# Weight rests kept in the ring, four first columns per input chunk, and products into an unread bank during the norms

## The reference

```
h = h + gate * rms_norm(mixer(modulate(rms_norm(h)))) 
h = h + gate * rms_norm(w_out @ (silu(g) * u))        # [g, u] = w_in @ modulate(rms_norm(h))
```

## Time and profile before

| | |
|---|---|
| median of 3 runs | 2438.59 us (2438.23 to 2444.41) |
| the profiled execution | 2446.78 us, span 2445.0 us |
| PE busy | 2272.3 us, 93% of the span |
| PE weight loads, beside the products | 2079.2 us |
| DVE busy | 1587.0 us, 65% |
| ACT busy | 1100.2 us, 45% |
| POOL busy | 127.4 us, 5% |
| mean granted TensorE clock | 0.968 |

### The profile page before, as it was taken

The page is one execution under the profiler, slowest core; times in us unless marked ns, Lnnn a source line. Parts: engine busy times, 40 slices in busy tenths (PEclk is TensorE's granted clock), DMA queues, the critical chain, the costliest instruction groups (busy, mean ns, idle before and its releaser), DMA issues.

```text
span 2445.0 us, 40728 instructions
## 1 busy us (share of the span) xinstructions
PE 2272.3 (93%) x17218; PEld 2079.2 (85%) x17218; DVE 1587.0 (65%) x2599; ACT 1100.2 (45%) x1711; POOL 127.4 (5%) x130
## 2 busy tenths in 40 slices
PE   6998999999979999989998989998999998989997
PEld 2664878998769998979998879997678998988997
DVE  3388666646955545886556575557967656687555
ACT  2424444444164346644335453334545334836333
POOL 0013000000000000000000000005620000000000
PEclk9999999999979999999999889999999999999999
DMA  7358164552225554314453225542034553513551
GB/s 324 121 215 317 55 231 148 190 186 86 75 103 190 180 183 155 138 70 173 179 183 138 104 100 189 181 152 87 1 116 148 184 190 139 189 52 121 183 181 67
DMA packets 50293, 368.41 MB, mean 151 GB/s; under 512 B 5568, under 2 KB 5696, under 8 KB 5824
## 3 DMA queue, kind: packets, MB, share of 16 engines
q1 hardware_dynamic: 49968, 363.72, 40.9%
q10 hardware_dynamic: 144, 2.10, 0.2%
HBM read 364.75 MB, written 1.05 MB: 150 GB/s over the span
## 4 chain that ended last, share of the span: by engine, by line
PE 79%; DVE 14%; ACT 3%; issue 3%; DMA 1%; SPq 0%; DVEq 0%; ACTq 0%
PE psum L240 67%; DVE weight_parts L226 2%; PE psum L3722 1%; PE psum L3723 1%; DMA weight_ring<-stream_dram 1%; PE psum L2532 1%; DVE work L998 1%; DVE work L2839 1%; DVE work L993 1%; ACT weight_parts L197 1%; DVE work L2853 1%; PE psum L3740 1%; DVE work L2841 1%; PE psum L3017 1%; PE psum L2205 1%
## 5 line engine op out<-in xcount | busy, mean ns | idle before, releaser
L240 PE MATMUL psum<-input_parts,weight_parts 128*128 128x256 f32 x8640 | 1062.8, 286 | 45.3 <-DVE input_parts L1006 29.1
L240 PEld LDWEIGHTS psum<-input_parts,weight_parts 128*128 128x128 f32 x8640 | 1055.4, 193 | 55.3 <-issue 48.7
L226 DVE TENSOR_TENSOR weight_parts<-weight_ring,weight_parts 128x1024 fp32r<-128x1024 f32 x536 | 631.7, 1220 | 268.1 <-ACT weight_parts L197 267.1
L197 ACT ACTIVATE weight_parts<-weight_ring 128x1024 fp32r<-128x1024 f32 x540 | 541.2, 1051 | 270.0 <-PE psum L240 269.2
L240 PE MATMUL psum<-hidden_parts,weight_parts 128*128 128x256 f32 x3744 | 455.3, 283 | 10.5 <-DVE hidden_parts L2658 6.6
L240 PEld LDWEIGHTS psum<-hidden_parts,weight_parts 128*128 128x128 f32 x3744 | 449.4, 189 | 14.3 <-issue 8.8
L1080 ACT ACTIVATE work<-psum 128x256 f32<-128x256 f32 x132 | 50.7, 384 | 427.7 <-PE psum L240 427.7
L1087 DVE TENSOR_TENSOR work<-work,psum 128x256 f32<-128x256 f32 x132 | 55.6, 421 | 287.6 <-ACT work L1080 287.6
L240 PE MATMUL psum<-work,weight_ring 128*128 128x256 f32 (+1 forms) x608 | 174.8, 446 | 4.0 <-ACT work L540 2.2
L240 PEld LDWEIGHTS psum<-work,weight_ring 128*128 128x128 f32 x608 | 117.4, 195 | 57.9 <-issue 41.9
L240 PE MATMUL psum<-weight_ring,silu_cond 128*32 128x256 f32 x768 | 53.6, 408 | 25.3 <-DMA weight_ring<-stream_dram 19.3
(11 more groups left out here) (459 smaller groups left out, 2230.5 us busy)
## 6 DMA issues: line engine op xcount, KB each, us to landing
weight_ring<-stream_dram SPq DMA_DIRECT2D x341, 1024.0 KB, 4.8
constants<-constants_dram SPq DMA_DIRECT2D x1, 2304.0 KB, 14.6
work<-s_bc_dram ACTq DMA_DIRECT2D x1, 2048.0 KB, 8.1
work<-ctx_dram SPq DMA_DIRECT2D x1, 1024.0 KB, 7.1
residual<-x_dram SPq DMA_DIRECT2D x1, 1024.0 KB, 9.1
out_dram<-residual SPq DMA_DIRECT2D x1, 1024.0 KB, 3.9
vectors<-vectors_dram SPq DMA_DIRECT2D x1, 550.5 KB, 3.8
constants<-constants_dram SPq DMA_DIRECT2D x1, 64.0 KB, 3.5
```

The lines of the kernel that those rows point to most:

```text
L197: act.activation(self.parts[:, s % SPLITS, 0, cols], self.ring[:, i % RING, cols], ACT.Identity)\
L226: return dve.tensor_tensor(self.parts[:, s % SPLITS, 1, cols], self.ring[:, i % RING, cols], self.parts[:, s % SPLITS, 0, cols].bitcast(F3 ...
L240: mm = pe.matmul(*args, **kw)
```

## The change

The high parts of four slabs now stand in `weight_parts`, and the rest of a slab stands in a second tensor at the same place as the ring (`weight_rest`): it overwrites the slab that it is made from. A ring place is free when PE has used the slab, no longer when it is split. Rounding and splitting run two slabs ahead (`last + 2`, `slab0 + n + 2`), and the stages no longer split the next stage's slabs after or inside a norm.

`first_columns` opens two slabs together and computes four columns from each input chunk. It is now used at the start of `GateUp`, `HgrnIn`, `MlstmIn`, `S5In` and of every output projection of eight chunks but the one with a gate. Where two columns share a bank later (`pair`), the first columns take two banks (`job_in_two_banks`). The input chunks are scaled and lowered one by one, no longer in pairs.

In the norms PE computes products of constants into `mod_bank` (`idle_products`, L380 of the changed kernel), which nobody reads: two after the sums, one after the variance is taken, one or two after the root. The last norm and `ConformerNorm` have none.

In the output projection after hgrn, mlstm and hgrn again, in the hybrid's readout and in `ConformerNorm`, the next two slabs are split by POOL. The convolution's last chunk has 15 taps on PE instead of 8. `ConformerNorm` takes mean and squares chunk by chunk from shifted values, as `NormedProjection` does, so that the sum is ready with the last chunk.

```
...
-SPLITS = 2
+SPLITS = 4
...
+        return self.open(pe, 1)[0]
+
+    def open(self, pe, n):
+
+        first = self.at
+        self.release, self.held = self.held, n
+        self.at += n
+        return [self.terms(pe, i) for i in range(first, first + n)]
+
+    def terms(self, pe, i):
+
         if i in self.split_slabs:
             s = self.split_slabs.index(i)
-            pe.wait_ge(self.split_done, s + 1)
-            return self.parts[:, s % SPLITS, 0, :], self.parts[:, s % SPLITS, 1, :]
+            pe.wait_ge(*self.ready(i))
+            return self.parts[:, s % SPLITS, :], self.rest[:, i % RING, :]
         pe.wait_ge(self.loaded[i % RING], 16 * (i // RING + 1))
         return self.ring[:, i % RING, :],
 
+    def ready(self, i):
+        return self.split_done, self.split_slabs.index(i) + 1
...
-        if i in self.split_slabs:
-            return self.split_done, self.split_slabs.index(i) + 1
         return self.used, i + 1
...
+    def leave_to_pool(self, last):
+
+        slabs = self.leave(last)
+        self.on_pool += slabs
+        return slabs
...
+            i = self.split_slabs[s]
+            if s > 0 and (s in self.on_pool) != (s - 1 in self.on_pool):
+                dve.wait_ge(self.split_done, s)
+            for half in range(2):
+                cols = slice(half * SLAB // 2, (half + 1) * SLAB // 2)
+                dve.wait_ge(self.rounded, 2 * s + half + 1)
+                ins = dve.tensor_tensor(self.rest[:, i % RING, cols], self.ring[:, i % RING, cols],
+                                        self.parts[:, s % SPLITS, cols].bitcast(F32), ALU.subtract)
+            ins.then_inc(self.split_done, 1)
...
+    def job_in_two_banks(self, free):
+
+        early = self.claim(free)
+        job = self.job(free)
+        job.early = early
...
+def idle_products(k, pe, n):
+
+    if not k.mod_bank_idle:
+        pe.wait_ge(*k.background.ready)
+        k.mod_bank_idle = True
+    for _ in range(n):
+        pe.matmul(k.mod_bank[:, 0:T], k.c("ident"), k.c("lower_pairs", 0, T), start=True, stop=True)
...
         mm.then_inc(self.job.full[0], 1)
+        idle_products(self.k, pe, 2)
+        pe.wait_ge(*self.root)
+        idle_products(self.k, pe, 2)
...
-        first = [(0,), (1,)] if self.chunks == KC else [(0, 1)]
-        self.groups = first + [(2, 3), (4, 5), (6,), (7,)]
+        first = [(0,), (1,), (2,), (3,)] if self.chunks == KC else [(0, 1), (2, 3)]
+        self.groups = first + [(4, 5), (6,), (7,)]
...
+def first_columns(k, pe, x, x_ready, columns, order):
+
+    for job, half in columns:
         begin(pe, job)
-    slab = [s.rearrange("p (k c) -> p k c", k=KC) for s in k.weights.next(pe)]
+    slabs = [[s.rearrange("p (k c) -> p k c", k=KC) for s in terms] for terms in k.weights.open(pe, 2)]
     for at, c in enumerate(order):
-        pe.wait_ge(*stage.x_ready[c])
-        for i, job in enumerate(jobs):
-            mm = k.weights.product(pe, job.ap[:, 0:T], [s[:, c, i * P:(i + 1) * P] for s in slab],
-                                   [x[:, c, :] for x in stage.x], at == 0, at == KC - 1)
-            if at == KC - 1:
+        pe.wait_ge(*x_ready[c])
+        for i, (job, half) in enumerate(columns):
+            mm = k.weights.product(pe, job.ap[:, half * T:(half + 1) * T],
+                                   [s[:, c, i % 2 * P:(i % 2 + 1) * P] for s in slabs[i // 2]],
+                                   [part[:, c, :] for part in x], at == 0, at == KC - 1)
+            if at == KC - 1 and job.full:
...
+        if self.next_slab < k.weights.count:
+            idle_products(k, pe, 2)
+            pe.wait_ge(*self.var_taken)
+            idle_products(k, pe, 1)
+            pe.wait_ge(*self.root)
+            idle_products(k, pe, 2 if self.split else 1)
...
-            if not early and not (after and g[0] == KC - 1) and g[0] != KC - 2:
-                k.weights.split_through(dve, last + 1)
+            if g[0] != KC - 2:
+                k.weights.split_through(dve, min(last + 2, self.next_slab - 1) if self.after else last + 2)
...
-        if after:
-            k.weights.split_through(dve, self.next_slab)
+        if self.after:
+            self.for_pool = k.weights.leave_to_pool(self.next_slab + 1)
...
+        for c in range(KC):
+            if c in (4, 6):
+                chain.link(centre(c))
+            scale(c)
+            if c >= 1:
+                lower(c - 1)
+        lower(KC - 1)
...
-                for i in range(PE_TAPS):
-                    at = DVE_TAPS + i
-                    mm = pe.matmul(job.ap[:, 0:T], self.taps[:, c % 2, i, :], self.u[:, c, at:at + T],
-                                   start=(i == 0), stop=(i == PE_TAPS - 1))
+                first = self.first_tap(c)
+                for at in range(first, CONV_C):
+                    mm = pe.matmul(job.ap[:, 0:T], self.tap(c, at), self.u[:, c, at:at + T],
+                                   start=(at == first), stop=(at == CONV_C - 1 and c < SHIFTED))
+                if c >= SHIFTED:
+                    pe.wait_ge(*self.shifted)
+                    mm = pe.matmul(job.ap[:, 0:T], k.c("ident"), self.shift, start=False, stop=True)
...
+        self.square(act, 0, SHIFTED)
+        for c in range(SHIFTED, KC - 1):
+            self.square(act, c, 1)
+        k.weights.round_through(act, self.next_slab + 1)
+        self.square(act, KC - 1, 1)
...
```

More of the change, by code:

```diff
@@ L729, in lower @@
+            if self.split and c >= 2:
+                self.lower(dve, c - 2)
+        dve.wait_ge(*self.h_new[-1])
+        if self.split:
             dve.wait_ge(*self.parts_ready[-1])
+    def lower(self, dve, c):
+        dve.wait_ge(*self.hi_ready[c])
+        dve.tensor_tensor(self.parts[1][:, c, :], self.k.h[:, c, :], self.parts[0][:, c, :].bitcast(F32),
+                          ALU.subtract).then_inc(self.parts_ready[c][0], 1)
 LATE = 4
-def first_columns(stage, pe, jobs, order):
-    k = stage.k
-    for job in jobs:
+def first_columns(k, pe, x, x_ready, columns, order):
+    for job, half in columns:
@@ L757, in __init__ @@
         self.pause_at = chunks if chunks == KC else 2 * chunks // 3
+        self.after = chunks == KC and not glu
         super().__init__(core)
@@ L899, in scalar @@
         act.activation(self.mean_sq, self.mean_job.ap[:, 0:T], ACT.Square).then_inc(self.mean_squared[0], 1)
-        if not early and self.split:
-            k.weights.round_through(act, self.next_slab + 1, halves=1, left=self.out_jobs[-1].full)
         act.wait_ge(*self.var_taken)
@@ L929, in vector @@
         y, sq = self.y, self.sq
-        early = len(self.x) == 1 and self.split
-        after = self.chunks == KC and not self.glu
         for e in self.h_old:
@@ L955, in vector @@
                 chain.link(dve.tensor_tensor(sq[:, 0, :], sq[:, 0, :], sq[:, 1, :], add))
-                if not early and not after:
-                    k.weights.split_through(dve, last + 1)
-            if early and g[0] < KC - 1:
-                k.weights.split_through(dve, self.next_slab + self.ahead(g))
+                if not self.after:
+                    k.weights.split_through(dve, last + 2)
             for i, c in enumerate(g):
@@ L2556, in scalar @@
                 self.make_taps(act, j + 1)
+            if j == SHIFTED:
+                act.wait_ge(*self.shift_job.full)
+                act.activation(self.shift, self.shift_job.ap[:, 0:T], ACT.Copy, scale=-KC / 2.0)\
+                   .then_inc(self.shifted[0], 1)
     def vector(self, dve):
@@ L2717, in pair, with two_banks, copy_columns @@
     return job.ap[:, :].rearrange("p (a t) -> p a t", a=2)
+def two_banks(jobs):
+    return [column for job in jobs for column in ((job.early, 0), (job, 1))]
+def copy_columns(act, job, out):
+    if job.early is job:
+        return act.activation(out, pair(job), ACT.Identity)
+    act.activation(out[:, 0, :], job.early.ap[:, 0:T], ACT.Identity)
+    return act.activation(out[:, 1, :], job.ap[:, T:2 * T], ACT.Identity)
 class HgrnIn(Stage):
```

374 lines of the change are left out of this document (196 added, 178 removed).

## The result

| | before | changed kernel |
|---|---|---|
| median | 2438.85 us (4 runs) | 2418.5 us (2416.79 to 2423.52, 4 runs) |
| the profiled execution, its span | 2446.78, 2445.0 | 2417.26, 2415.5 |
| PE busy | 93% | 2279.1 us, 94% |
| POOL busy | 127.4 us | 179.3 us |
| mean granted TensorE clock | 0.968 | 0.985 |

The ratio is 0.9919 (95% interval 0.9902 to 0.9936), 20.4 us by the medians: faster by 0.8%. So the traces are compared stage by stage.

A forecast was written before the change was run, and what follows sets the result against it. PE, busy 93% of the span, was taken as the bound. Terms A to G sum to +54.3 us, H takes 30.6, net +23.7: from 2438.6 to 2414.9 us, range 2382 to 2434.

The forecast's parts named there:

- DVE and POOL by turns: Case that DVE operations with both operands in SBUF wait for POOL's splits; chance 0.45, own range 2405 to 2425.
- A: Stage starts: four columns a chunk and idle products in norms end DVE's pacing and mostly keep PE's clock; +32.0 us.
- The rival built on it: Clock not held in the starts despite idle products, so practically no change, 2442.7 us; chance 0.12.
- B: First input chunk after a norm lowered behind two scales, not four: 0.6 us earlier at seven starts; +4.2 us.
- D: No split in front of the variance on DVE in the norms of three projections; +2.4 us.
- C: Rounding two slabs ahead removes about one in five of PE's late-split waits in the projections; +3.8 us.
- E: Float32 starts, S5's four slabs and the conformer's two, come nearer full speed; +3.8 us.
- F: ConformerNorm: seven taps moved from DVE to PE and sums ready with the last chunk; +11.7 us.
- H: Twenty split halves moved to POOL hold up DVE in conformer, three projections and readout; -30.6 us.
- G: Three projections: a DVE split between second and third column makes PE wait 1.2 us each; -3.6 us.
- Nothing on PE waits for them: Claim that PE waits for none of the twenty split halves on POOL, their slabs being needed only after the norm.
- The ring: Slower rival: PE holds ring places longer, loads start later and slabs come late; 2449 us, chance 0.05.

The follow-up runs named there:

- e4: The kernel before with the idle products alone, at the same places as in the changed kernel; 2437.2 us, ratio 0.9996 to the kernel before.
- e1: The changed kernel without its idle products in the norms; 2429.7 us, ratio 0.9966 to the kernel before.
- e6: The changed kernel with the conformer norm's two slabs split by DVE after its last tap instead of by POOL; 2408.6 us.
- e2: The changed kernel with the next two slabs split by DVE instead of POOL in the output projections after hgrn, mlstm and hgrn; 2401.5 us.
- e8: e2 with POOL subtracting constants from constants, into an area nobody reads, at the moments it split before; 2422.1 us.
- e9: e2 with POOL doing memsets, which only write SBUF, at the moments it split before; 2396.6 us.

## Why the prediction was right, and where not

The forecast was 2415, it came to 2418.5, inside the forecast's own range and the wider one; the likeliest case, DVE and POOL by turns, is the one that happened. By its steps:

- **A, size right (33.5 for 32), reason wrong.** The step that failed is "elapsed time times (1 - granted clock) gives how much of it is clock". The stretch was bounded by DVE, and the clock's loss lay under that wait: e4 restores the clock in six starts and they stay at 82.9 us for 83.5. The clock's own worth was 14.1 us, and only with DVE's pace away; the forecast had 24 of its 32 in it. "If the clock still falls, the pace alone gives 8" failed with it; e1 gives 19.4. The rival built on it, 2442.7, would have come out as e1's 2429.7. That 32 came so near 33.5 is luck.
- **B and D** held but for the size. PE after the first hgrn's projection, in the changed kernel:

```profile
1081.27 0.59 PE L884 MATMUL psum<-work,constants 128*128 128x256 f32 x2
1081.70 1.55 PE L380 MATMUL psum<-constants 128*128 128x256 f32 x6
1083.54 1.13 PE L380 MATMUL psum<-constants 128*128 128x256 f32 x4 [0.29 <-ACT work L925]
1085.41 0.48 PE L242 MATMUL psum<-input_parts,weight_parts 128*128 128x256 f32 x2 [0.75 <-DVE input_parts L1022]
```

  From the start of the last sum to the first product it is 4.14 us where it was 5.49, 1.35 for the forecast's 1.4. The ten instructions between are the five idle products. After mlstm it is the same; after the second hgrn it is 0.86, since PE is at half clock at these sums (0.85 us each for 0.43). The three starts after a projection of 22 chunks won 0.54, 0.52 and 0.52, and that of S5 0.17. Together 5.3 for 6.6.
- **C** was mis-sized. The waits in the last columns went, but five others of 1.36 came at the third slab, behind ACT's residuals. Waits for splits went from 10.6 to 8.3: 2.3 for 3.8. Where a moved rounding would stand in ACT's queue wasn't looked up.
- **E**: the chain of the changed kernel has the two starts with 27.88 and 14.05 us where it had 30.60 and 15.64, 4.3 for 3.8.
- **F with H in the conformer**: from the end of the input's first two slabs to the output projection it is 89.9 us where it was 93.8, 3.9 for 2.9. But both terms were off, and that they met is luck. Going by turns stretched DVE by 8.4, near the 8.8 priced, and only 3.4 of it were on the path (e6), for PE had its own sums until 667. So F alone was worth 7.3, not 11.7: its sum has DVE's path, and PE's 14 sums behind its last tap, 6.0 us, stand in no term of it.
- **G and H in the projections**: 14.3 + 7.9 = 22.2 us of waits for the forecast's 3.6 + 21.3. L997 and L998 were stretched by 1.60 and 2.02 for 1.6 and 2.3. ("Waiting for a whole POOL operation" said more than the earlier trace rows show: the longest L1523 is 0.80 over its median, a copy takes 1.34.) G was 1.2 a time to the digit (e2). The price of the second slab isn't POOL's alone: with DVE's own split there the early sums still wait 6.7. Not forecast was that PE falls to half clock behind such a wait, 6.0 us.
- **"Nothing on PE waits for them"** failed in the readout, where PE waits 1.5 us for POOL's second slab. But before it waited as long there, for DVE's split. What the readout lost is 0.8: its sums over the partitions now wait 0.84 us for ACT (L2413), where nothing waited before.
- **The ring** starved nobody. PE's waits for a transfer of weights are those of the first block, 19.4 us in seven places, and landing takes 4.8 as before.

The sum by rows: 33.5 + 5.3 (B, D) + 2.3 + 4.3 + 3.9 - 22.2 - 6.0 - 0.8 (readout) = 20.3. The medians give 20.4, but that doesn't confirm the sum: its rows come from the two profiled executions, which differ by 29.5. So 9.2 us of them stand in no term. The largest piece is in mlstm: from its first product to the start of its output projection the stage fell by 10.4 us, 5.6 of them in its first 96 products, and the granted clock there went from 0.89 to 0.95. How much of this the change does and how much differs between executions of one kernel isn't shown.

The Trainium skill, page SBUF — State Buffer, section "Who interferes with whom", says that a DVE instruction with two SBUF inputs contends with a GpSimd instruction that reads SBUF and not with one that only writes. The measurements agree: 2.00 us beside POOL's reads in e8, 0.42 beside its writes in e9, and 0.42 for L990 with one operand in PSUM in the middle of a POOL split.

## What to carry to other kernels

A low clock is worth something only where the engine is the bound of that stretch: before pricing it, look whether PE waits for its producer at full clock too. Work moved to POOL cost DVE nothing here beside DVE operations with an operand in PSUM, and beside POOL's memsets of e9 even those with both in SBUF kept their length; beside DVE operations with both operands in SBUF, POOL's splits of 9.9 us cost it 8.4. The cheaper place may be a gap of DVE itself. When work is moved two steps ahead, look up what each queue holds in front of its first new place.

## What the runs showed of the hardware

Not expected: with a single PE wait of 4.8 us within a projection come 6.8, 6.8 and 3.4 us at half clock, which begin in its last us or at its end (0.77 over the 11.24 us behind the first). With the wait at 1.2 us (e2) the clock stays at 1.00 there. Four or five products in a norm of about the same length leave the next start at 1.00, nine times of nine, where without them (e1) it is 0.81 to 0.89. POOL's reads hold DVE across different tensors: its constants against DVE's split of the ring, 3.94 us for two halves that take 2.36.
